# Small vectors loaded from ScalarE's queue, and the first key projection paced by quarters of w_mk

## What is computed

```python
def memory_kv(mem, norm_mem_g, w_mk, w_mv, mk_norm_g):
    h = rmsnorm(mem, norm_mem_g)
    n, m = mem.shape[:2]
    k = rmsnorm((h @ w_mk).reshape(n, m, MEM_HEADS, MEM_HEAD_DIM), mk_norm_g)
    v = (h @ w_mv).reshape(n, m, MEM_HEADS, MEM_HEAD_DIM)
    return k, v
```

## Time and profile before

| what | us |
|---|---|
| median of three timed runs | 1611.09 |
| lowest and highest of them | 1607.86, 1616.06 |
| the profiled execution, its own time | 1617.55 |
| its span in the trace | 1615.7 |
| its mean granted TensorE clock | 0.923 of full speed |

### The profile page before, as it was taken

How to read it: one execution, slowest core, us unless ns; L and a number is a source line. 1 busy time by engine, 2 the same in 40 slices (tenths; PEclk the granted TensorE clock), 3 DMA queues, 4 the chain that set the end, 5 groups by cost and what they waited for, 6 DMA issues and landing times.

```text
span 1615.7 us, 14074 instructions
## 1 busy us (share of the span) xinstructions
PE 1332.2 (82%) x4830; PEld 708.9 (44%) x4830; DVE 788.7 (49%) x2066; ACT 235.8 (15%) x560; POOL 174.4 (11%) x228
## 2 busy tenths in 40 slices
PE   4988888988989847788999999984399999999980
PEld 2434444544445423443555555552244444444440
DVE  0206989999899892222323233223512144352545
ACT  0112222222122110111111111110001101101110
POOL 0000001100100001000000000000000122221304
PEclk9998899999999968798999999987599999999995
DMA  7683000200000111461114010022159999999936
GB/s 297 226 301 105 1 20 34 97 27 27 1 27 14 62 67 46 169 234 60 40 48 160 26 39 14 14 91 97 62 171 328 320 350 348 328 360 340 356 138 203
DMA packets 131073, 228.09 MB, mean 141 GB/s; under 512 B 17096, under 2 KB 95862, under 8 KB 130979
## 3 DMA queue, kind: packets, MB, share of 16 engines
q1 hardware_dynamic: 115819, 207.24, 36.9%
q0 software_dynamic: 14608, 17.87, 3.4%
q10 hardware_dynamic: 576, 2.10, 0.3%
HBM read 218.36 MB, written 45.25 MB: 163 GB/s over the span
## 4 chain that ended last, share of the span: by engine, by line
PE 64%; DVE 24%; issue 4%; DMA 3%; ACT 2%; POOL 1%; SPq 1%; DVEq 0%; ACTq 0%; POOLq 0%
PE bank L696 19%; PE bank L1066 14%; DVE W L1441 11%; PE bank L1037 8%; PE bank L1072 8%; PE bank L884 3%; PE bank L1010 2%; PE bank L966 2%; PE bank L1061 2%; DVE G L1830 1%; DVE W L1480 1%; DVE G L1387 1%; DVE st L1490 1%; DVE W L1509 1%; POOL st L579 1%
## 5 line engine op out<-in xcount | busy, mean ns | idle before, releaser
L696 PE MATMUL bank<-W,G 128*128 128x512 f32 (+3 forms) x992 | 413.7, 576 | 9.7 <-DMA W<-in_w_mk 6.6
L696 PEld LDWEIGHTS bank<-W,G 128*128 128x128 f32 (+1 forms) x992 | 185.6, 190 | 217.5 <-issue 210.0
L1441 DVE SCALAR_TENSOR_TENSOR W<-W,dwT 128x128 f32<-128x128 f32 (+1 forms) x1080 | 281.0, 338 | 0.0
L1066 PE MATMUL bank<-W 128*128 128x512 f32 x528 | 234.0, 596 | 1.7 <-DVE W L1816 1.7
L1066 PEld LDWEIGHTS bank<-W 128*128 128x128 f32 x528 | 100.8, 191 | 128.8 <-issue 126.4
L884 PE MATMUL bank<-W 128*128 128x512 f32 (+1 forms) x288 | 130.1, 611 | 10.4 <-DVE W L1549 7.0
L1072 PE MATMUL bank<-W 128*128 128x512 f32 x264 | 122.1, 605 | 15.6 <-ACT W L1339 15.6
L1037 PE MATMUL bank<-W 128*128 128x512 f32 (+1 forms) x288 | 133.4, 623 | 0.6 <-DVE W L1652 0.6
L575 POOL TENSOR_SCALAR st<-st 128x1 f32<-128x1 f32 (+5 forms) x58 | 15.0, 259 | 1018.8 <-DVE st L1516 328.5
L1816 DVE TENSOR_TENSOR W<-bank,cvec 128x512 f32<-128x512 f32 x66 | 42.6, 686 | 141.8 <-PE bank L1061 141.8
L1830 DVE SCALAR_TENSOR_TENSOR G<-W,dwT,G 128x1024 f32<-128x1024 f32 (+1 forms) x72 | 92.2, 1281 | 18.8 <-issue 13.2
(11 more groups left out here) (257 smaller groups left out, 1181.3 us busy)
## 6 DMA issues: line engine op xcount, KB each, us to landing
W<-in_w_exp_gate SPq DMA_DIRECT2D x33, 1024.0 KB
W<-in_w_exp_up SPq DMA_DIRECT2D x33, 1024.0 KB
W<-in_w_exp_down SPq DMA_DIRECT2D x33, 1024.0 KB
y_scratch<-W SPq DMA_DIRECT2D x33, 512.0 KB, 4.4
y_scratch<-LG SPq DMA_DIRECT2D x1, 8192.0 KB
W<-in_cache_mem_k SPq DMA_DIRECT2D x8, 1024.0 KB, 5.0
W<-in_cache_mem_v SPq DMA_DIRECT2D x8, 1024.0 KB, 7.0
W<-in_w_in SPq DMA_DIRECT2D x4, 1792.0 KB, 24.5
```

What stands on the lines that cost most here:

```text
L696: mm = pe.matmul(bank[0:rows, at:at + hi - lo], HT[:, c, 0:rows], w[:, c, lo:hi], start=(c == 0), stop=(c == DC - 1))
L1066: mm = pe.matmul(B[2 + par][:, :], HG[par][:, c, :], WGU[u][:, c, :], start=(c == 0), stop=(c == DC - 1))
L1441: dve.scalar_tensor_tensor(y, src, w, y, ALU.mult, ALU.add).then_inc(M["conv_tap"], 1)
```

## The change

The 16 small loads move, unchanged and in the same order, from SP's function to the head of ScalarE's, ahead of its first wait. SP then issues `cst`, the two memory tiles and w_mk at once. w_mk's four quarters get a semaphore each (`wmk_in`, a ring of 4). TensorE's key projection is written out with the blocks of 128 rows outside and the two banks inside; for the first memory tile it waits ahead of every second block for the quarter that holds it. The second memory tile has the same order of products, without those waits. The wait for all 16 small loads ahead of TensorE's first transpose stays.

```diff
         @block.sync
         def _(sp):
             kc = i["consts"]
             sp.dma_start(cst[:, :], kc[:, 0:256]).then_inc(M["c_in"], 16)
-            small = 0
-            r = 0
-            for name, n in (("norm_mix_g", 8), ("norm_xa_g", 8), ("norm_mem_g", 8), ("norm_ffn_g", 8),
-                            ("conv_dw_b", 4), ("conv_ln_g", 4), ("conv_ln_b", 4)):
-                sp.dma_start(STAGE[r:r + n, :], i[name][0].rearrange("(c p) -> c p", p=128)).then_inc(M["small_in"], 16)
-                r += n
...
-                sp.dma_start(dst, i[name].to_broadcast([128, n])).then_inc(M["small_in"], 16)
             mem = i["mem_prompt"][0]
             for m in range(2):
                 sp.dma_start(XR[m], mem[m * 128:(m + 1) * 128, :]).then_inc(x_in[m], 16)
-            load_rows(sp, w_mk, i["w_mk"][0], M["wmk_in"])
+            for c in range(4):
+                sp.dma_start(w_mk[:, 2 * c:2 * c + 2, :], i["w_mk"][0].rearrange("(c p) n -> p c n", p=128)[:, 2 * c:2 * c + 2, :]).then_inc(wmk_in[c], 16)
             load_rows(sp, w_mv, i["w_mv"][0], M["wmv_in"])
...
                 turn_z(m, 128)
                 pe.wait_ge(M["ht_ready"], 2 * m + 2)
-                if m == 0:
-                    pe.wait_ge(M["wmk_in"], 64)
-                else:
+                if m:
                     pe.wait_ge(M["mk_normed"], 2)
-                for half in range(2):
-                    project(B[2 + half], 512 * half, 512 * half + 512, w_mk, 128).then_inc(M["mk_done"], 1)
+                for c in range(DC):
+                    if m == 0 and c % 2 == 0:
+                        pe.wait_ge(wmk_in[c // 2], 16)
+                    for half in range(2):
+                        mm = pe.matmul(B[2 + half][:, :], HT[:, c, :], w_mk[:, c, 512 * half:512 * half + 512], start=(c == 0), stop=(c == DC - 1))
+                        if c == DC - 1:
+                            mm.then_inc(M["mk_done"], 1)
...
         @block.scalar
         def _(act):
+            r = 0
+            for name, n in (("norm_mix_g", 8), ("norm_xa_g", 8), ("norm_mem_g", 8), ("norm_ffn_g", 8),
+                            ("conv_dw_b", 4), ("conv_ln_g", 4), ("conv_ln_b", 4)):
+                act.dma_start(STAGE[r:r + n, :], i[name][0].rearrange("(c p) -> c p", p=128)).then_inc(M["small_in"], 16)
+                r += n
...
+            for dst, name, n in ((GMK, "mk_norm_g", MHD), (gk_bc[:, :], "k_norm_g", HD), (sink_bc[:, :], "attn_sinks", HEADS),
+                                 (br_bc[:, 0:NG], "b_router_group", NG), (br_bc[:, NG:36], "b_router_expert", NE)):
+                act.dma_start(dst, i[name].to_broadcast([128, n])).then_inc(M["small_in"], 16)
+
             act.wait_ge(M["vec_tdone"], 1)
```

More of the change, by code:

```diff
@@ L255, in ring @@
             return [sem(f"{name}{r}") for r in range(n)]
-        M = {n: sem(n) for n in """c_in small_in wmk_in wmv_in win_in wout_in wmq_in wmo_in dist_in wr_in skv_in rconst_in
+        M = {n: sem(n) for n in """c_in small_in wmv_in win_in wout_in wmq_in wmo_in dist_in wr_in skv_in rconst_in
             moved_out vec_tdone vec_ready mhalf_ready mean_eps
@@ L324, in build @@
         x_in, x1_in, x1_out, x2_out = ring("x_in", 4), ring("x1_in", 4), ring("x1_out", 4), ring("x2_out", 4)
+        wmk_in = ring("wmk_in", 4)
         mk_in, mv_in = ring("mkb_in", 2), ring("mvb_in", 4)
@@ L1136, in _ @@
         def _(act):
+            r = 0
[3 more added lines that the diff above has]
+                r += n
+            for half in range(2):
+                act.dma_start(STAGE[V_GQ:V_GQ + 1, 64 * half:64 * half + 64], i["q_norm_g"]).then_inc(M["small_in"], 16)
+            act.dma_start(STAGE[V_MQ:V_MQ + 2, :], i["mq_norm_g"][0].rearrange("(c p) -> c p", p=128)).then_inc(M["small_in"], 16)
+            act.dma_start(DWS[0:TAPS, :], i["conv_dw_w"][0]).then_inc(M["small_in"], 16)
+            for dst, name, n in ((GMK, "mk_norm_g", MHD), (gk_bc[:, :], "k_norm_g", HD), (sink_bc[:, :], "attn_sinks", HEADS),
+                                 (br_bc[:, 0:NG], "b_router_group", NG), (br_bc[:, NG:36], "b_router_expert", NE)):
+                act.dma_start(dst, i[name].to_broadcast([128, n])).then_inc(M["small_in"], 16)
             act.wait_ge(M["vec_tdone"], 1)
```

## The result

The changed kernel took 1621.86 us, the median of ten runs (1618.54 to 1627.32), against 1612.49 for ten runs of the kernel before beside it: a ratio of 1.0053 (95% interval 1.0036 to 1.0069), 9 us or half a per cent slower. Its profiled execution took 1623.88 us for a span of 1622.1, at a mean granted clock of 0.919; before it was 1615.7 at 0.923, so the two spans lie 6.4 us apart.

A forecast was written before the change was run, and what follows sets the result against it. TensorE was taken as the bound, its opening waiting for w_mk until 25.07; after the change late small loads (20.0) plus 7.03 us preparation start the projection at 27.1, +2.0 us: median 1613.1, range 1604 to 1621.

The forecast's parts named there:

- What bounds the opening, and that one arm's gain is not used: Opening: loads and preparation meet at the first key product; the load side gains 4 to 7 us, none used.
- The load arm: SP's consts, memory rows and w_mk: memory rows issued 5.90 us earlier; w_mk's last large packet at 20.8 beside small loads.
- ScalarE's issues: Sixteen small-load issues on ScalarE's queue start at 0.72 and end near 6.6; slower issue could add 3 us.
- Turns by packet, one to one: On the shared DMA engines, SP's and ACT's queues alternate single packets; a large packet takes 0.158 us.
- first packet 1.7 us after it, as now: 5.7: conv_dw_w's load, issued at 4.03, sends its first packet 1.7 us later, as in the kernel before, at 5.7.
- The 40 behind: 6.8: Five broadcasts' 40 packets behind conv_dw_w on its engine: 6.3 us of turns plus 0.5 for their own bytes, ending at 20.0.
- Sum: Small loads in at 20.0, h at 27.0, projection start at 27.1 instead of 25.07: +2.0 us.
- TensorE's slow opening: TensorE's first records at 0.81 against 0.41 us each from 29.9 on; it moves with the start, priced at no difference.
- Signs of being wrong: First transpose starting by 13 or after 30, or the first key-projection product still waiting for a w_mk load.
- (a): Small loads not held up on the DMA engines: in at 11.7, start 18.8, 6.3 us faster, median 1604.8; chance 0.27.
- (b): DMA queues take turns of a whole load's share of an engine: start at 49.5, 24 us slower, 1635.5; chance 0.08.
- (c): Something between, a change that shows nothing: small loads in at 18, start at 25, 1611; chance 0.10.

The follow-up runs named there:

- e4: Changed kernel with conv_dw_w's 31-row load issued as two loads of 16 and 15 rows; 1615.20 us, ratio 1.0009.
- e7: Changed kernel with each conv_dw_w row written as two halves of 1024 B, 62 packets instead of 31; 1625.39 us, one run.
- e3: Changed kernel with SP waiting for all 16 small loads before issuing memory rows and w_mk; 1607.38 us, one run.
- e10: Changed kernel with ten same-shaped loads of 8-byte rows beside the small loads, the real large loads issued only after all are in; 1611.22 us, one run.
- e13: Changed kernel with ScalarE waiting for memory tile 0 before issuing its sixteen small loads; 1623.26 us, one run.
- e6: Changed kernel with w_mk and w_mv issued as eight loads of 512 KB each instead of four of 1 MB; 1618.11 us, one run.
- e8: Changed kernel with all loads on SP's queue in order of need, conv_dw_w split, five broadcasts last, pacing kept; 1604.33 us, ratio 0.9939.
- e12: The kernel with all loads on SP's queue in order of need, run again in more rounds; 1602.87 us, ratio 0.9929 against the kernel before.

## Why the forecast's direction held and its size did not

- **What bounds the opening, and that one arm's gain is not used.** Right. The load arm came in 11 us ahead of h (20.7 against 31.8), TensorE waited for L1392 and not for w_mk, and 7.00 us of preparation followed the small loads (7.03 forecast).
- **The load arm.** Right: last quarter of w_mk in at 20.7 against 20.8 beside the small loads.
- **ScalarE's issues.** They ended at 7.98 instead of 6.6, the last five taking 0.46 to 0.75 each; inside the 3 us allowed, and hidden, since the last load waited for its turn and not for its issue.
- **Turns by packet, one to one.** Right, shown by 402 against 402 packets, by e4 and by e7. The taps' 31 x (0.083 + 0.158) = 7.5 us stand: they ran from 9.26 to 16.55, 7.3 us.
- **The step that failed: "first packet 1.7 us after it, as now: 5.7".** The lag between conv_dw_w's issue and its first packet was taken over from the kernel before, where nothing large ran beside it. I applied the company of the large loads to the taps and to what is behind them, and not to what is ahead. In the changed kernel the first packet came at 9.26, 4.8 us after its issue at 4.46: 3.6 of the missing 4.7 us. e3 (1.0 us alone) and e10 (0.9 beside as many packets of 8 bytes) show that the large loads' bytes make this lag, and e13 (3.6) that it outlasts their start.
- **"The 40 behind: 6.8".** Mis-sized by 0.9 us: from 16.55, where the taps end, to the last packet's end at 24.24 are 7.7. What the term leaves out are the small writes that raise the semaphores, which take turns as packets too: one behind the taps and one behind each broadcast. From the last packet to the landing at 24.72 that the chain shows are 0.5 more, also left out.
- **Sum.** Small loads in at 24.7 instead of 20.0 (3.6 - 0.2 + 0.9 + 0.5, rounded), product at 31.86 instead of 27.1: +6.8 instead of +2.0. TensorE's slow opening, priced at no difference, gave back 0.8 (5.96 left at the keys). The span rose by 6.4. The medians differ by 9.4, with 5.8 to 11 in the interval, which holds the 6.0 of the time line; what the medians show beyond it no run explains.
- **Signs of being wrong.** None of the three that were set came: the transpose at 24.86 lies between 13 and 30, and the product waited for VectorE. They left too wide a gap to catch this miss.
- **Rivals.** (a), no hold-up, fell: the transpose was at 24.86, not 11.7. (b), whole shares, fell with 402 to 402. (c), small loads in at 18, missed by more than the forecast did. The chances named the right case; its own range, 1609 to 1621, lacked a bound for the loads ahead.

What stays open: what the lag between issue and first packet is made of, and why the first four loads take until 7 in the changed kernel. e10 shows that it depends on the large loads' bytes, e6 that their size as loads matters little, e13 that it is no cost of their start alone; what makes it no run tells.

## What to carry to other kernels

When small loads are moved to a second queue so that bulk loads can start sooner, count every packet that the small ones put on their fullest engine, semaphore writes and those ahead of the critical one as well, price each at one large packet's time, and add the lag from issue to first packet as it is beside the bulk traffic (3.6 to 4.8 us here, 1.0 alone); a load whose row count spreads badly (31 rows) is the first to split. If the small loads gate the work, as they do here, order is worth more than parallel queues: send what is needed first alone, then the bulk, then what is needed late. Waiting by quarters pays only on the arm that is late, so find that arm with the other edits in place.

## What the runs showed that I had not expected

- One load of 62 KB cut into 16 and 15 rows instead of 31 lands everything behind it 6.20 us sooner beside bulk traffic (e4), although alone the 31 packets take only 2.6 us.
- While another queue moves large rows at over 400 GB/s, the first packet of a short load comes 3.5 us after its issue (e13, 5.06 to 8.53), 1.0 alone (e3). Once they run, short loads pass at about 0.4 us each.
- A write of 4 bytes that raises a semaphore takes a turn of its own, 0.16 us here, as a packet of data does.
- The same kernel gives profiled spans of 1600.5 (e8, clock 0.921) and 1607.7 (e12, clock 0.919) with the same opening, products at 14.24 and 14.28: some 7 us that no edit made. Another run of e12 had a span of 1601.2 at 0.919, so the mean clock alone does not tell them apart. A shift of a few us is read from the time line's anchors and not from two spans.
